# Branch merge of a hybrid transformer: each block product made as three products of high and low parts, with the merge and the output product by halves

## The reference, cut to what matters

```python
# hybrid_mixer, run twice (layers 0 and 1)
y_dn = o.reshape(B, S, DN_V).astype(h.dtype) @ w_up_dn          # 256x1024 @ 1024x1024
y_sb = o_sb.reshape(B, S, SB_W).astype(h.dtype) @ w_up_sb       # 256x512  @ 512x1024
g_dn, g_sb = jnp.split(jax.nn.sigmoid(gates), N_BRANCH, axis=-1)
return (g_dn * y_dn + g_sb * y_sb) @ w_out                      # 256x1024 @ 1024x1024
```

## Time and profile before

| | |
|---|---|
| median of 3 runs | 3916.58 us (3913.28 to 3918.37) |
| the profiled execution, its own time | 3912.89 us |
| its span from first to last instruction | 3911.1 us |
| layer 0, stage of the merge | about 440.9 to 521.6 us of the span |
| layer 1, stage of the merge | about 1188.3 to 1269.0 us |
| second mixer, stage of the merge | about 2877.5 to 2969.2 us |

### The profile page before, as it was taken

How to read it: one execution, slowest core, us unless ns; L and a number is a source line. 1 busy time by engine, 2 the same in 40 slices (tenths; PEclk the granted TensorE clock), 3 DMA queues, 4 the chain that set the end, 5 groups by cost and what they waited for, 6 DMA issues and landing times. The chain is left out here.

```text
span 3911.1 us, 53939 instructions
## 1 busy us (share of the span) xinstructions
PE 3551.5 (91%) x21361; PEld 3103.5 (79%) x21361; DVE 2435.9 (62%) x3003; ACT 1821.9 (47%) x1987; POOL 56.0 (1%) x36
## 2 busy tenths in 40 slices
PE   4988889989798699999999996798598899999999
PEld 4978779989687477777877776797377899977887
DVE  6847246468451388888888873453533688596665
ACT  3534234344331367767667652353222444464554
POOL 0000000000000000000000000000000000000000
PEclk9999989999999799999999998899799899999999
DMA  6730236458011299999999972353013455503554
GB/s 221 257 126 6 108 130 238 171 179 310 12 66 44 86 347 364 360 362 362 364 363 361 360 278 97 108 194 119 7 55 108 162 182 182 181 25 122 192 193 159
DMA packets 296865, 739.01 MB, mean 189 GB/s; under 512 B 17449, under 2 KB 17904, under 8 KB 291312
## 3 DMA queue, kind: packets, MB, share of 16 engines
q1 hardware_dynamic: 296688, 736.60, 53.4%
HBM read 735.50 MB, written 1.05 MB: 188 GB/s over the span
## 5 line engine op out<-in xcount | busy, mean ns | idle before, releaser
L1930 DVE TENSOR_TENSOR weight_ring_low<-weight_ring,weights_high 128x2048 fp32r<-128x2048 f32 x336 | 773.5, 2344 | 149.8 <-ACT weights_high L1876 149.8
L1876 ACT ACTIVATE weights_high<-weight_ring 128x2048 fp32r<-128x2048 f32 x336 | 618.3, 1908 | 7.7 <-DMA weight_ring<-in_moe_w 7.7
L374 PE MATMUL psum_all<-h_high_projections,high_projections 128*128 128x256 f32 x1536 | 440.8, 287 | 25.5 <-DVE h_low_projections L309 25.4
L374 PE MATMUL psum_all<-h_low_projections,high_projections 128*128 128x256 f32 x1536 | 437.0, 285 | 0.0
L374 PE MATMUL psum_all<-h_high_projections,weight_ring_low 128*128 128x256 f32 x1536 | 432.2, 281 | 0.0
L1818 PE MATMUL psum_all<-weights_high,expert_in_turn_high 128*128 128x512 f32 x896 | 359.8, 402 | 17.7 <-DVE weight_ring_low L1930 11.6
L1818 PE MATMUL psum_all<-weights_high,expert_in_turn_low 128*128 128x512 f32 x896 | 356.9, 398 | 0.0
L1818 PE MATMUL psum_all<-weight_ring_low,expert_in_turn_high 128*128 128x512 f32 x896 | 352.0, 393 | 0.0
L374 PEld LDWEIGHTS psum_all<-h_high_projections,high_projections 128*128 128x128 f32 x1536 | 292.7, 191 | 30.1 <-DVE h_low_projections L309 30.0
L374 PEld LDWEIGHTS psum_all<-h_high_projections,weight_ring_low 128*128 128x128 f32 x1536 | 296.9, 193 | 0.0
L2818 PE MATMUL psum_all<-peer_h_high,expert_rows_high 128*128 128x256 f32 x1024 | 291.1, 284 | 5.0 <-DVE expert_rows_low L2866 5.0
(11 more groups left out here) (591 smaller groups left out, 7453.5 us busy)
## 6 DMA issues: line engine op xcount, KB each, us to landing
weight_ring<-in_moe_w SPq DMA_DIRECT2D x336, 1024.0 KB, 5.1
weight_ring<-in_w_in SPq DMA_DIRECT2D x48, 2048.0 KB, 8.5
expert_rows<-in_peer_down SPq DMA_DIRECT2D x128, 512.0 KB, 3.3
expert_rows<-in_peer_up SPq DMA_DIRECT2D x128, 512.0 KB, 3.3
weight_ring<-in_ffn_halves SPq DMA_DIRECT2D x42, 1024.0 KB, 6.9
branch_out<-in_ada_w SPq DMA_DIRECT2D x64, 512.0 KB, 9.8
weight_ring<-in_w_out SPq DMA_DIRECT2D x6, 2048.0 KB, 7.9
weight_ring<-in_ada_w SPq DMA_DIRECT2D x4, 2048.0 KB, 11.7
```

The lines of the kernel that those rows point to most:

```text
L374: mm = pe.matmul(half(k.ps, 4 * (g % R) + j), w[:, c, j * P:(j + 1) * P], x[:, c], start=(c == 0 and n == 0), stop=(c == KC - 1 and n == 2))
L1876: act.activation(high[:, q, h * HALF:(h + 1) * HALF], k.ring[:, q, h * HALF:(h + 1) * HALF], ACT.Copy).then_inc(high_made[q], 1)
L1930: dve.tensor_tensor(k.low[:, q, part], k.ring[:, q, part], high[:, q, part].bitcast(F32), ALU.subtract).then_inc(low_made[q], 1)
```

## The change

`branches` gets the split form of the product. For every source and every panel ScalarE makes a high part and VectorE a low part; each half panel has its own signal. The function `three` makes three fp32r matmuls where one 32-bit matmul was. The last branch is merged in two halves of four blocks, and the output's first panel is multiplied first with blocks 0 to 3 of `merged`, then with blocks 4 to 7; the output's blocks go to every second place in PSUM. In the second mixer the order of the branches becomes dilated, memory, ssd, and three panels of high parts are kept (H = 3) where the layers keep two. The high parts of the weights lie in memory of `projected` that is no longer needed.

```diff
@@ branches, scalar
+                def source(i, c0, c1):
+                    act.activation(source_high[:, at[i] + c0:at[i] + c1], parts[i][1][:, c0:c1], ACT.Copy).then_inc(source_made, 1)
+
+                def split(p, n):
+                    g = panels[p][0]
+                    act.wait_ge(k.loaded[g % R], k.value[g])
+                    if p >= H:
+                        act.wait_ge(k.used, g - H + 1)
+                    act.activation(high[:, p % H, part(p, n)], k.ring[:, g % R, part(p, n)], ACT.Copy).then_inc(high_made, 1)
+                for m, (c0, c1) in enumerate(pieces(0)):
+                    source(0, c0, c1)
+                    split(0, m)
+                if len(pieces(0)) < 2:
+                    split(0, 1)
+                for i in range(1, len(parts)):
+                    for c0, c1 in pieces(i):
+                        source(i, c0, c1)
+                split(1, 0)
+                split(1, 1)
+                if H > 2:
+                    split(2, 0)
+                    split(2, 1)
                 for i in range(len(parts)):
                     act.activation(gate_of(i), gate_of(i), ACT.Sigmoid).then_inc(opened, 1)
+                for p in range(H, n_all - 1):
+                    split(p, 0)
+                    split(p, 1)
+                for n in range(2):
+                    act.wait_ge(taken, len(parts) + n)
+                    act.activation(merged_high[:, 4 * n:4 * n + 4], merged[:, 4 * n:4 * n + 4], ACT.Copy).then_inc(merged_made, 1)
+                split(n_all - 1, 0)
+                split(n_all - 1, 1)
@@ branches, tensor
+                    for n, (w, x) in enumerate(((w_hi, hi), (w_hi, lo), (w_lo, hi))):
+                        mm = pe.matmul(out, w, x, start=start and n == 0, stop=stop and n == 2)
...
+                        for m in range(len(group)):
                             for j in range(4):
                                 for c in range(KC):
-                                    mm = pe.matmul(place(i, 4 * m + j), w[:, c, j * P:(j + 1) * P], src[:, c],
-                                                   start=(c == 0), stop=(c == KC - 1))
+                                    if j == 0 and c % 4 == 0:
+                                        pe.wait_ge(low_made, 2 * p + c // 4 + 1)
+                                        if m == 0:
+                                            pe.wait_ge(source_split, n_pieces[i] + c // 4 + 1)
+                                    mm = three(place(i, 4 * m + j), p, c, slice(j * P, (j + 1) * P), KC, src_hi[:, c], src_lo[:, c],
+                                               c == 0, c == KC - 1)
                             mm.then_inc(k.used, 1)
-                pe.wait_ge(taken, len(parts))
+                            p += 1
+                pe.wait_ge(taken, len(parts) - 1)
                 for m in range(2):
+                    if m == 1:
+                        pe.wait_ge(taken, len(parts) + 1)
+                    for c0 in (0, 4):
+                        pe.wait_ge(low_made, 2 * p + c0 // 4 + 1)
+                        if m == 0:
+                            pe.wait_ge(merged_split, c0 // 4 + 1)
+                        for j in range(4):
+                            for c in range(c0, c0 + 4):
+                                mm = three(result(m, j), p, c, slice(j * P, (j + 1) * P), KC, merged_high[:, c], merged_low[:, c],
+                                           c == 0, c == KC - 1)
                     mm.then_inc(k.used, 1)
@@ branches, vector
+                def merged_part(n):
+                    dve.wait_ge(merged_made, n + 1)
+                    dve.tensor_tensor(merged_low[:, 4 * n:4 * n + 4], merged[:, 4 * n:4 * n + 4], merged_high[:, 4 * n:4 * n + 4].bitcast(F32),
+                                      ALU.subtract).then_inc(merged_split, 1)
+                next_low = [1]
+                for m in range(len(pieces(0))):
+                    source(0, m)
+                    low(0, m)
+                if len(pieces(0)) < 2:
+                    low(0, 1)
+                for i in range(1, len(parts)):
+                    for m in range(len(pieces(i))):
+                        source(i, m)
+                lows(H)
...
+                for i, (group, _) in enumerate(parts[:last]):
+                    lows(p + H if group[0][1] else p + len(group) - 1 + H)
+                    p += len(group)
+                    dve.wait_ge(k.used, first + p)
+                    dve.wait_ge(opened, i + 1)
+                    branch(i, slice(0, 8))
+                group = parts[last][0]
+                lows(p + 2)
+                if group[0][1]:
+                    dve.wait_ge(made, 1)
+                else:
+                    dve.wait_ge(k.used, first + p + 1)
+                dve.wait_ge(opened, last + 1)
+                branch(last, slice(0, 4))
+                lows(min(p + 3, n_all - 1))
+                merged_part(0)
+                dve.wait_ge(k.used, first + p + len(group))
+                branch(last, slice(4, 8))
+                merged_part(1)
+                lows(n_all)
@@ second_mixer
-        branches(k, "branches2", [([(s["br_ssd"], None), (s["br_ssd"] + 1, None)], k.o[:, 0:8]), ([(s["br_dil"], 2)], k.o[:, 8:10]),
-                                  ([(s["br_mem"], 3), (s["br_mem"] + 1, 3)], k.o[:, 10:16])], (G20, G20 + 8, G20 + 16), s["out2"], None)
+        branches(k, "branches2", [([(s["br_dil"], 2)], (k.o[:, 8:10], k.o_at + 8 * 4 * T)),
+                                  ([(s["br_mem"], 3), (s["br_mem"] + 1, 3)], (k.o[:, 10:16], k.o_at + 10 * 4 * T)),
+                                  ([(s["br_ssd"], None), (s["br_ssd"] + 1, None)], (k.o[:, 0:8], k.o_at))],
+                 (G20 + 8, G20 + 16, G20), s["out2"], None, H=3)
```

More of the change, by code:

```diff
@@ L1366, in gate_of, with place, result, width @@
                 return k.proj[:, gates[i]:gates[i] + 8]
+            def place(i, j):
+                return half(k.ps, 8 * (i % 2) + j)
+            def result(m, j):
+                return half(k.ps, 8 * ((len(parts) + m) % 2) + 2 * j)
+            def width(p):
+                kb = panels[p][1]
+                return HALF if kb is None else kb * D // 2
+            def part(p, n):
+                return slice(n * width(p), (n + 1) * width(p))
+            def pieces(i):
+                return [(c, min(c + 4, parts[i][1].shape[1])) for c in range(0, parts[i][1].shape[1], 4)]
@@ L1368, in _ @@
+            n_pieces = [sum(len(pieces(m)) for m in range(i)) for i in range(len(parts) + 1)]
             @block.scalar
             def _(act):
+                def source(i, c0, c1):
[19 more added lines that the diff above has]
+                    split(2, 1)
@@ L1376, in _, with three @@
+                split(n_all - 1, 0)
+                split(n_all - 1, 1)
             @block.tensor
             def _(pe):
-                for i, (panels, src) in enumerate(parts):
+                def three(out, p, c, cols, kb, hi, lo, start, stop):
+                    g = panels[p][0]
+                    w_hi = high[:, p % H, 0:2 * width(p)].rearrange("p (c n) -> p c n", c=kb)[:, c, cols]
+                    w_lo = k.low[:, g % R, 0:2 * width(p)].rearrange("p (c n) -> p c n", c=kb)[:, c, cols]
+                    for n, (w, x) in enumerate(((w_hi, hi), (w_hi, lo), (w_lo, hi))):
+                        mm = pe.matmul(out, w, x, start=start and n == 0, stop=stop and n == 2)
+                    return mm
@@ L1379, in _ @@
+                p = 0
+                for i, (group, x) in enumerate(parts):
                     if i >= 2:
                         pe.wait_ge(taken, i - 1)
[L1381 to L1388, removed]
+                    src_hi = source_high[:, at[i]:at[i] + x.shape[1]]
+                    src_lo = source_low[i]
+                    last = i == len(parts) - 1
+                    if group[0][1]:
+                        pe.wait_ge(source_split, n_pieces[i + 1])
+                        pe.wait_ge(low_made, 2 * (p + len(group)))
+                        total = x.shape[1]
@@ new lines, in low, with lows @@
+                def low(p, n):
+                    g = panels[p][0]
+                    dve.wait_ge(high_made, 2 * p + n + 1)
+                    dve.tensor_tensor(k.low[:, g % R, part(p, n)], k.ring[:, g % R, part(p, n)], high[:, p % H, part(p, n)].bitcast(F32),
+                                      ALU.subtract).then_inc(low_made, 1)
+                def lows(upto):
+                    while next_low[0] < upto:
+                        low(next_low[0], 0)
+                        low(next_low[0], 1)
+                        next_low[0] += 1
```

86 lines of the change are left out of this document (50 added, 36 removed).

## The result

The changed kernel takes 3881.64 us (median of 4 runs, 3879.74 to 3885.37) against 3914.93 of before: a ratio of 0.9919, 95% interval 0.9905 to 0.9933. The forecast was 3881. In a second set of runs it took 3882.98 against 3914.88, ratio 0.9916 (0.9903 to 0.993).

What follows compares the result with a forecast made beforehand. TensorE was taken to set the merge stages, plus 4.71 us of merge and 2 us at the end. -13.4 x 2 - 9.4 = -36 us gave 3876.9 profiled, 3881 median; range 3869 to 3893, 3866 to 3896 with rivals.

Steps and rivals of the forecast that it cites:

- The product: Block products in the merge stages: 0.353 us split instead of 0.434, 0.080 saved on each, 41 us in all.
- The start, layers: Start of each layer's merge: first matmul after 5.35 us of copies and low part, then a wait of 0.8 us.
- The clock at the start, layers: Slow products at 1.2 GHz at the start of each layer's merge: net against before -0.5 us.
- The merge, layers: Ahead of each layer's output product: gap 0.4 us instead of 4.71 (-4.3), and no clock fall after it (-1.95).
- The second mixer: Its merge stage: later start, slow products, a 3.1 us wait and late ssd halves against cheaper products: -9.4 us.
- The pauses and the clock: Two pauses at the second mixer's start let the clock fall: 2.3 and 1.3 us of slow products.
- Late hand-off: At the merge, ScalarE or VectorE becomes the bound: 19 us more, 3900 us; chance 0.12.
- The clock staying down: TensorE starts in pieces and the clock stays at its lower level through the first branches: 3955 us; chance 0.05.
- Rival 3: The clock staying down: each slow product costs 0.29 us more, 124 beyond the count cancel the gain; 3955 us, chance 0.05.
- windows at 0.50 beyond 12 us of a stage: Sign in the PE clock of the merge stages that would show the clock staying at its lower level.
- rival 4: The three matmuls run as 32-bit ones, 0.434 us each: 445 us more, 4326 us; chance 0.01.
- The total: Two layers at -13.4 us and the second mixer at -9.4: -36 us, median 3881 us.

Runs made afterwards that it cites:

- the split made ahead: Changed kernel with the first up_dn panel of each layer's merge split into high and low parts in the stage before (delta_norm): 3877.01 us.
- ssd first: Changed kernel with the second mixer's branches in the old order (ssd, dilated, memory), three panels of high parts kept: 3888.82 us.
- idle products: Changed kernel with small products on constants (ten in a layer, sixteen in the second mixer) while TensorE waits at each merge's start: 3877.88 us.
- the last three versions: Changed kernel with first panel split ahead plus idle products, 3875.04 us; first panel ahead plus ssd's source parts after the memory panels', 3870.82; all three edits, 3873.53.
- the split work with 32-bit products: Changed kernel with all its splitting, but one 32-bit product of the high parts in place of three fp32r products: 3915.24 us.

## Why the prediction was right, by its own steps

- **The product.** 0.080 us less each: measured 0.4338 - 0.3553 = 0.0785, 40 us on 512. Right. Three of the four passes that the Trainium skill gives for a true FP32 product (FP8 and Floating Point Precision, TensorE Precision Notes) would have taken 0.325, an estimate from that page, and the trace doesn't agree: 0.355. That the products carried the gain alone would be a wrong reading: with the products but without the halves the stages are 8.6 us shorter, with the halves but without the products 20.4, with both 34.9.
- **The start, layers.** 5.35 us and a wait of 0.8: measured 5.23 and 0.41. Right, with 0.5 us less than forecast, and the split made ahead shows that it is on the path (3.55 us back).
- **The clock at the start, layers.** -0.5 us forecast. Measured: the first 64 products end at 475.81 (VectorE's gate of branch 0), 26.0 us after 449.79, less 0.41 of wait and 64 x 0.355 = 22.7: 2.9 us lost to the lower clock, where 2.7 were lost before. So +0.2. A mis-sized term: the clock was at 0.50 for 2.6 us after the pause (453.13 to 455.8) instead of the one to two taken, and with the 2.9 us ahead of it that makes 5.5 us of slow work. Part of this is chance, as the layers' scatter shows (3.4 to 6.0 us until the clock is up).
- **The merge, layers.** A gap of 0.4 us, measured 0.31, by the sequence foretold: out panel's low parts to 482.4, half merge to 484.9. The clock stayed up: out's first panel took 11.58 us (1224.67 to 1236.25). Gap and clock together were forecast at 6.25 us; measured 4.4 for the gap and 1.8 for the clock (15.86 - 13.88 before, 11.58 - 11.37 now), 6.2. Sum of a layer: -12.6 + 5.2 + 0.4 + 0.2 - 4.4 - 1.8 = -13.0, measured -12.8 and -12.9. The sum fits in part by luck: the start came 0.5 us better and the clock 0.7 worse than forecast.
- **The second mixer.** Start 4.2, measured 4.11 (2860.59 - 2856.48). Memory products 15.2 us in, measured 14.80. ssd's two late halves 1.6 us, measured 9.9 - 5.92 - 2.55 = 1.4. Sum -9.4, measured -9.12. One step was phrased in a way that misleads: the 2.3 us for dilated's slow products and the 3.1 of pause were two terms, but only their sum with the products is fixed, by VectorE's queue. I took the first to be recoverable by a higher clock in an experiment, and it wasn't.
- **The pauses and the clock.** The warning of the Trainium skill (TensorE: Matmul & The Clock Gate, Why this matters for your kernels) against pauses between bursts held in the second mixer, although this pause is shorter than those that the page warns of: after 2.55 us of it came 3.4 us at 0.50, some 1.5 us lost, for the 1.3 of the forecast.
- **The rivals.** Late hand-off: did not occur; the 0.9 us of slack in the layers held. The clock staying down: it was up 6.0 us after the first product in layer 0. Rival 3 needed 124 slow products beyond the forecast's count of 26 (7.5 in each layer, 11 in the second mixer); there were about 29, eight in each layer and 13 in the second mixer. Yet the sign that the prediction named for it, windows at 0.50 beyond 12 us of a stage, did appear: 15.9 to 19.3 us into the second mixer's, behind the pause that the forecast itself had from 12 to 15 us, with slow products of its own after it. The sign was badly chosen. And rival 4's time has a slip: three matmuls of 0.434 us in place of 0.353 for all three come to 0.95 x 512 = 486 us on 3881, 4367 and not 4326.
- **The total.** Stages -34.9 for -36.2 forecast; timed -33.3 and, in the second set (whose stages are 35.4 shorter than before's), -31.9. The 1.6 and 3.5 us between the stages and the medians are of the size of the remainder's scatter and weren't settled: whether the changed kernel's start times tend to put the other stages on their longer lengths stays open, since its own two profiles had a long remainder (3663.8 and 3666.1), as the one with the panel split ahead (3666.0) and with ssd first (3663.6), while idle products alone had 3657.8 and the last three versions 3661.1, 3652.8 and 3658.0.

## What to carry to other kernels

When a product gets cheaper, count the hand-over ahead of it as well: here the split lengthened it from 4.7 to 7.2 us, and without merging by halves three quarters of the gain (26.3 of 34.9 us) would have been lost. When an engine waits, find whose queue ends the wait, and take work out of that queue; speeding up the waiting engine only made the pause longer here, and in the second mixer it cost the clock as well. Compare stages, not only totals, where small stages of an untouched part come in two lengths.

## What the hardware showed that was not expected

- The same 16 small matmuls took 5.40 or 7.19 us, by whether the granted clock fell from 1.00 to 0.50 during them or ahead of them; the sum of the untouched stages scattered over 13 us (3652.8 to 3666.1).
- A pause of 2.55 us (after), 2.52 us and 4.79 us (with idle products) ahead of the memory products was followed by windows at 0.50; with a pause of 0.29 us, and with one of 1.10 (the split work with 32-bit products), the clock stayed at 1.00. That was worth about 1.5 us, beside the 2.3 us of work taken out of VectorE's queue.
- In after, the clock fell about 1.1 us after the products had begun again (2871.28, at 1.00 until 2872.4), so the row of a restart doesn't yet tell at which level the burst will run.
